# A hybrid decoder layer on one core: two activation chunks split early beside the last up panels, and a weight load queued two panels later

## The reference

```python
h = rms_norm(x, norm_mix); proj = h @ w_in
# three mixers: sparse attention with compressed blocks (A), state space (B), stick-breaking (C)
k_cmp = rms_norm(einsum('bnlhd,hlde->bnhe', k_blocks, cmp_wk), k_gain[0])   # mixer A
v_cmp = einsum('bnlhd,hlde->bnhe', v_blocks, cmp_wv)
x = x + merged @ w_out
u = rms_norm(x, norm_ffn) @ w_up                  # 1024 -> 2 * 2048
u = causal_depthwise_conv_width_3(u) + conv_b
gate, val = split(u, 2); x = x + (gelu(gate) * val) @ w_down   # 2048 -> 1024
```

## Time and profile before

| | |
|---|---|
| Median of 3 runs | 1601.62 us (1597.72 to 1611.2) |
| The profiled execution | 1610.47 us, of which the span is 1608.7 us |
| PE busy | 1506.2 us (94%) |
| DVE, ACT, POOL busy | 679.5, 357.3, 474.5 us |
| Mean granted clock of TensorE | 0.954 |
| DMA | 76.46 MB, mean 48 GB/s |
| The up projection's stream on PE | about 1074 to 1422 us of the span |
| The down projection | 1429 to 1605 us |

### The profile page before, as it was taken

One profiled execution on the slowest core, in us unless ns is written; L12 is line 12 of the kernel. 1 busy time (PEld: TensorE's weight loads), 2 busy tenths in 40 slices (PEclk: granted clock), 3 DMA queues, 4 the chain that ended last, 5 costly groups with the idle time before them and its releaser, 6 DMA issues.

```text
span 1608.7 us, 18480 instructions
## 1 busy us (share of the span) xinstructions
PE 1506.2 (94%) x7493; PEld 1210.9 (75%) x7493; DVE 679.5 (42%) x1036; ACT 357.3 (22%) x622; POOL 474.5 (29%) x242
## 2 busy tenths in 40 slices
PE   5698899898999989999999988989999999989999
PEld 5588556567978777777778867878888888868887
DVE  5677554452263455444442250063323322354551
ACT  5211432231011013444330020051111111131110
POOL 4323001112345212011112433314433433434452
PEclk9898789999998979999999999989999999999999
DMA  7321100003111100000001104131111111131113
GB/s 168 41 35 30 40 0 14 1 1 79 35 50 33 33 17 18 17 17 17 17 17 33 46 13 158 53 131 53 40 52 52 40 51 52 49 133 53 53 41 116
DMA packets 127862, 76.46 MB, mean 48 GB/s; under 512 B 40352, under 2 KB 114464, under 8 KB 127776
## 3 DMA queue, kind: packets, MB, share of 16 engines
q1 hardware_dynamic: 127792, 75.46, 16.8%
HBM read 66.93 MB, written 8.52 MB: 47 GB/s over the span
## 4 chain that ended last, share of the span: by engine, by line
PE 85%; DVE 9%; ACT 2%; DMA 2%; issue 1%; POOL 1%; SPq 0%; ACTq 0%; DVEq 0%; POOLq 0%
PE ps L629 22%; PE ps L631 21%; PE ps L630 21%; PE ps L1100 3%; PE ps L1130 3%; PE ps L860 3%; PE ps L886 3%; PE ps L1114 2%; PE ps L874 1%; PE ps L644 1%; DVE arena L1477 1%; DMA raw<-in_w_out 1%; DVE hTl L1951 1%; PE ps L1058 1%; PE ps L1077 1%
## 5 line engine op out<-in xcount | busy, mean ns | idle before, releaser
L541 POOL TENSOR_TENSOR wh<-raw,zero 128x1024 fp32r<-128x1024 f32 (+1 forms) x94 | 189.1, 2011 | 1101.4 <-PE ps L631 1018.8
L629 PE MATMUL ps<-hTh,wh 128*128 128x512 f32 (+1 forms) x1024 | 412.1, 402 | 3.9 <-ACT arena L1312 3.1
L630 PE MATMUL ps<-hTl,wh 128*128 128x512 f32 (+1 forms) x1024 | 404.1, 395 | 0.0
L631 PE MATMUL ps<-hTh,wl 128*128 128x512 f32 (+1 forms) x1024 | 403.6, 394 | 0.0
L544 POOL TENSOR_TENSOR wl<-raw,wh 128x1024 fp32r<-128x1024 f32 (+1 forms) x94 | 259.4, 2759 | 7.4
L629 PEld LDWEIGHTS ps<-hTh,wh 128*128 128x128 f32 (+1 forms) x1024 | 194.1, 190 | 50.3 <-issue 6.5
L629 PE MATMUL ps<-wh,hTh 128*128 128x512 f32 (+1 forms) x576 | 207.5, 360 | 22.2 <-POOL wl L544 9.3
L631 PEld LDWEIGHTS ps<-hTh,wl 128*128 128x128 f32 (+1 forms) x1024 | 193.8, 189 | 43.4
L630 PEld LDWEIGHTS ps<-hTl,wh 128*128 128x128 f32 (+1 forms) x1024 | 194.1, 190 | 40.1
L630 PE MATMUL ps<-wl,hTh 128*128 128x512 f32 (+1 forms) x576 | 206.5, 358 | 0.0
L631 PE MATMUL ps<-wh,hTl 128*128 128x512 f32 (+1 forms) x576 | 206.3, 358 | 0.0
(11 more groups left out here) (310 smaller groups left out, 1569.7 us busy)
## 6 DMA issues: line engine op xcount, KB each, us to landing
raw<-in_w_in SPq DMA_DIRECT2D x37, 512.0 KB, 3.9
raw<-in_w_up SPq DMA_DIRECT2D x32, 512.0 KB, 4.0
raw<-in_w_down SPq DMA_DIRECT2D x16, 512.0 KB, 3.7
merged<-in_x SPq DMA_DIRECT2D x8, 512.0 KB, 7.3
raw<-in_w_out SPq DMA_DIRECT2D x8, 512.0 KB, 3.6
merged<-in_x SPq DMA_DIRECT2D x2, 2048.0 KB, 10.6
x_keep<-merged SPq DMA_DIRECT2D x2, 2048.0 KB, 9.7
conv<-x_keep SPq DMA_DIRECT2D x1, 2048.0 KB, 10.1
```

Of the source, the lines that this page charges most:

```text
L541: eng.tensor_tensor(wh[:, p, 0:n], raw[:, p, 0:n], zero1[:, 0:1].broadcast_to((P, n)), ALU.add).then_inc(s_hi[0], 1)
L629: mm(out_, ah, bh, start=first, stop=False, skip_group_check=True)
L630: mm(out_, ah, bl, start=False, stop=False, skip_group_check=True)
L631: return mm(out_, al, bh, start=False, stop=last, skip_group_check=True)
```

## The change

Three edits belong together. (1) A buffer pair `early_h`, `early_l` is laid in the place of `res1`. Its two chunks, cg 0 and 1, are split there on ACT and DVE between the seventh and the eighth pass over the pairs of up steps. The eighth pass is written out behind them on these two engines. The first down chunk on PE takes its activations from there, and its banks 0 to 3 wait only for the 30th `up_read`, banks 4 and 5 for the 31st, 6 and 7 for the 32nd. (2) The load of the residual, which overwrites `res1`, waits in addition for the first `dn_used`, the end of d = 0 on PE. (3) The compression weights come behind the load of panel P+2.

```diff
@@ program @@
+        early = ExitStack()
+        early_h = sb("early_h", [P, 2, L], F32R, at=early)
+        early_l = sb("early_l", [P, 2, L], F32R, at=early)
+        early.close()
         res1 = sb("res1", [P, TB, HALF], at=ffn)
@@ sync @@
-                if p == P_NSAPROJ:
+                if p == P_NSAPROJ + 2:
                     eng.wait_ge(S("pv_done"), NS)
...
                 if d == 3:
                     eng.wait_ge(S("act_done"), 16)
+                    eng.wait_ge(S("dn_used"), 1)
@@ tensor @@
-                            eng.wait_ge(S("up_read"), 32)
+                            eng.wait_ge(S("up_read"), 30 if tb < 4 else 31 if tb < 6 else 32)
...
-                        ins = mm3(ps[:, tb, :], hTh[:, cg % 8, t], hTl[:, cg % 8, t],
-                                  wh[:, d % 2, w], wl[:, d % 2, w], cg % 16 == 0, cg % 16 == 15)
+                        ah, al = (early_h[:, cg, t], early_l[:, cg, t]) if cg < 2 else (hTh[:, cg % 8, t], hTl[:, cg % 8, t])
+                        ins = mm3(ps[:, tb, :], ah, al, wh[:, d % 2, w], wl[:, d % 2, w], cg % 16 == 0, cg % 16 == 15)
@@ scalar @@
-            with eng.Fori(1, 8) as jj:
+            with eng.Fori(1, 7) as jj:
...
-            for cg in range(32):
+            for cg in range(2):
+                eng.wait_ge(S("act_done"), 14)
+                eng.activation(early_h[:, cg, :], act[:, cg, :], ACT.Copy).then_inc(S("dn_hi_x"), 1)
+            for u in range(2):
+                ffn_pair(7, u, False)
+            for cg in range(2, 32):
@@ vector @@
-            with eng.Fori(0, 8) as jj:
+            with eng.Fori(0, 7) as jj:
...
+            for cg in range(2):
+                act_low(cg)
+            for u in range(2):
+                ffn_pair(7, u)
...
-            for cg in range(22):
+            for cg in range(2, 22):
                 act_low(cg)
```

More of the change, by code:

```diff
@@ L1989, in _, with act_low @@
             eng.wait_ge(S("x2_saved"), 32)
-            with eng.Fori(0, 8) as jj:
+            def act_low(cg):
+                eng.wait_ge(S("dn_hi_x"), cg + 1)
+                high, low = (early_h[:, cg, :], early_l[:, cg, :]) if cg < 2 else (hTh[:, cg % 8, :], hTl[:, cg % 8, :])
+                tt(low, act[:, cg % 16, :], high.bitcast(F32), ALU.subtract).then_inc(S("dn_x"), 1)
+            with eng.Fori(0, 7) as jj:
                 for u in range(2):
                     ffn_pair(jj, u)
[L1994 to L1997, removed]
+            for cg in range(2):
+                act_low(cg)
+            for u in range(2):
+                ffn_pair(7, u)
             def y_out(g):
```

## The result

The changed kernel takes **1585.64 us** (median of 12 runs, 1582.67 to 1596.09); the kernel before, run beside it, 1604.07 (12 runs, 1597.45 to 1611.2). The ratio is **0.9894, interval 0.9873 to 0.9915**: 17 us faster, between 14 and 20 (the two medians stand 18.4 apart). The forecast was 1586.2 and 15.4 us. The gain is just over 1%, and the interval reaches to both sides of it. Three launches of later runs took 1641.69, 2132.06 and 2950.68 us and are left out of all ratios.

The account below looks back on a forecast made before the run. PE was taken to bound the kernel, holding 85% of the chain of waits. Gains of 6.8 and 8.6 us sum to 15.4, so 1601.6 - 15.4 = 1586.2 us; range 1578 to 1597.

Parts of the forecast that it names:

- Place A: PE going from panel P to P+1, after the attention: 6.8 us gained, 5.2 of stop and 1.6 of slow clock.
- the prediction's upper bound of twice 1.6: Slow clock behind the two stops: its share can be at most the same again, 18.5 us of gain in all.
- Place B: PE going from the up to the down projection: 8.6 us gained, 7.1 of stop and 1.5 of slow clock.
- The early split at no cost: Before the down projection: two ACT copies and two DVE subtractions, the latter within 6.81 us of DVE idleness, cost nothing.
- The prediction's 2.63 us for a subtraction beside POOL's split: DVE's subtractions for the down projection: 2.63 us each when POOL splits at the same time, 1.15 alone.
- The residual: Down projection: its load waits for d = 0; chunk 4's load behind it is there by 1452.9, costing 0.
- The rival's price: Down projection: chunk 4's load comes late behind the residual, PE stops; 1611 us at a landing at 1485; chance 0.04.
- Rivals 1 and 2: Place B only shrinks (bank 6 or chunk 1 late), 1590.5, chance 0.10; place A gives nothing, 1593.0, chance 0.10.
- The chance of "over 1%": Whole kernel: faster by over 1% (1% is 16.0 us) 0.41, within 1% 0.56, slower 0.03.

Follow-up runs that it names:

- The queue edit alone: The kernel before with only the compression weights' load moved two panels later in SP's queue: ratio 0.9952, interval 0.9923 to 0.9982.
- The bank experiment: The changed kernel, but its first down chunk waits for all banks (32nd `up_read`): ratio to the kernel before 0.9932, interval 0.9901 to 0.9963.

## Why the prediction was right

**Place A.** The sum had 5.2 us of stop and 1.6 of slow clock, 6.8 together. From the end of P to the end of P+1 it is 18.4 before and 11.6 after: 6.8. The queue edit alone shows it, and the slack was even larger than reckoned, since one panel would do. In other profiles of kernels with the old queue the same stop costs up to 8.0 (19.6 to 11.6): 5.2 of stop and 2.8 of slow clock, within the prediction's upper bound of twice 1.6.

**Place B.** 8.6 predicted, 8.5 measured (19.5 to 11.0), up to 9.8 in other profiles. The order of events came as laid out: chunk 0 went on one spacing after the last up matmul, banks 6 and 7 and chunk 1 were ready. The bank experiment shows the end of the taps as the next wait, 4.1 us behind the up projection. The clock's 1.5 us were rightly in the sum, though as a cause of its own it is worth 1.0: most of the rest would turn into a wait for a low half, which only the early split takes away.

**The early split at no cost.** Two subtractions in 2.36 us, then 2.99 us of idle time on DVE. Writing the pass out moved nothing that PE waits for: the up projection takes 378.9 us in both profiles. The product of the taps took 1.6 us in it where it took 1.2, but the 0.23 us idle ahead of it were gone, and PE did not wait for it. The prediction's 2.63 us for a subtraction beside POOL's split is a mean of two unequal ones: in the kernel before the first takes 1.92 us, and the second 3.41, until 1.1 us after POOL's subtraction has ended. None of this was needed at place B, where the first two ran alone.

**The residual.** Issued at 1414, chunk 4's load at 1419.3, which landed 10.8 us later (14.7 was reckoned at most); POOL never waited for it. The rival's price was worked out as a landing that must come later than 22 us after issue; the experiment issued the load later instead, and its own sum gave the stop and its cost within half a us.

**Rivals 1 and 2** did not occur: no stop at bank 6 or chunk 1, and the lead of place A is in the span up to the up projection (639.1 and 639.3 us from P+1 on).

**What the sum did not have.** It took the gain over from the profiled execution to the median, and that held within the interval. That the time itself came within 0.6 us, 1586.2 against 1585.64, is luck in part: the base of three runs, 1601.6, lay 2.4 us under the 1604.07 of twelve, and the medians moved 3.0 us more than the sum. And the two new profiles differed by 12.4 us more for the clock ahead of both edits; whoever checks the forecast of 15.4 on the spans finds 27.7 and could look for a third cause in the diff. The chance of "over 1%" was put at 0.41, and the measured middle lies at 1.06%: the runs can't tell the two sides of that line apart, as the prediction said. That the level of the clock makes most of the spread is likely from the stretches, not shown for the runs, and no experiment here fixed it.

## What to carry to other kernels

A transfer that must wait for a late event belongs in an in-order queue behind every load that is free to go; count how many loads stand behind it, and when each is wanted. At a seam between two stages of PE list all waits of the first matmul with their ends and shift work until the last of them is covered; of two that overlap, removing the one that ends first gives nothing. And compare the stretches of two profiles before their spans: what differs ahead of the first edited instruction is not the edit's.

## What was not expected of the hardware

- TensorE's clock stood at its lower level for some 30 us in one execution of the same instructions and not in another (0.51 and 1.00 over 170 to 190 us), 11 to 15 us of time between two profiles of one stretch; the runs of the kernels run more than once spread over 9 to 17 us.
- It fell to 0.50 at 165 us behind ten us in which PE was 93% busy, with no wait of more than 0.7 us among those of PE over 150 to 170 us.
- POOL could start on a 512 KB load 14.0 us after its issue behind two of 2 MB on the same queue, near the 14.7 of the earlier trace rows at another place; three loads of the same size in the down projection of the kernel before landed after 3.7.
- VectorE's subtraction with both operands in SBUF took 1.15 us alone; of two that met POOL's split the first took 1.92 and the second 3.41, and POOL's subtraction 3.25 where it takes 2.41 alone (kernel before, 1441 to 1448 us).
